# Delta rule's first step in early places and banks, key products shared through memory, and four couples at the feed-forward's entry

## The reference, cut to what matters

```python
kk = einsum("bnhcd,bnhsd->bnhcs", k, k)           # per chunk and head
a_mat = where(strict, beta[..., None] * kk * decay, 0)
t_mat = triangular_solve(eye + a_mat, eye)        # by blocks: 16, 32, 64, 128 here
qk = einsum("bnhcd,bnhsd->bnhcs", q, k) * decay
def step(state, xs):                              # one chunk after another, forward and backward
    v_new = u - w @ state
    o = q_c @ state + qk_c @ v_new
    state = state * exp(gl) + k_c.T @ v_new
h = h + concat([attn, gdn]) @ w_out
h = h + square(relu(rmsnorm(h) @ w_ffn_in)) @ w_ffn_out
```

## Time and profile before

| | |
|---|---|
| median of 3 runs | 2490.85 us |
| profiled execution | 2490.52 us |
| its span | 2488.7 us |
| TensorE busy | 2378.4 us (96%) |
| VectorE, ScalarE, GpSimd busy | 1424.9, 1031.3, 1042.4 us |
| granted clock, mean | 0.983 |

### The profile page before, as it was taken

How to read it: one execution, slowest core, us unless ns; L and a number is a source line. 1 busy time by engine, 2 the same in 40 slices (tenths; PEclk the granted TensorE clock), 3 DMA queues, 4 the chain that set the end, 5 groups by cost and what they waited for, 6 DMA issues and landing times. The chain is left out here.

```text
span 2488.7 us, 31195 instructions
## 1 busy us (share of the span) xinstructions
PE 2378.4 (96%) x11797; PEld 1902.7 (76%) x11797; DVE 1424.9 (57%) x1866; ACT 1031.3 (41%) x1748; POOL 1042.4 (42%) x647
## 2 busy tenths in 40 slices
PE   8999889998979999999999999999999999999986
PEld 6778778876857888878888777777777788877765
DVE  7754166555587555588667576666647441115854
ACT  5651144455244555544446243434333321015532
POOL 2112156453357666646767221212122342126553
PEclk9999999999998999999999999999999999999998
DMA  4113221115313444665553312111111452246462
GB/s 154 43 53 112 76 81 48 44 48 169 106 55 141 155 148 150 215 227 165 161 153 106 115 43 68 51 57 54 68 43 60 156 178 94 93 142 200 157 207 77
DMA packets 141202, 278.59 MB, mean 112 GB/s; under 512 B 26579, under 2 KB 36051, under 8 KB 141052
## 3 DMA queue, kind: packets, MB, share of 16 engines
q1 hardware_dynamic: 141052, 276.59, 33.3%
HBM read 200.18 MB, written 76.37 MB: 111 GB/s over the span
## 5 line engine op out<-in xcount | busy, mean ns | idle before, releaser
L1798 POOL TENSOR_TENSOR t<-t,t 128x512 fp32r<-128x512 f32 (+1 forms) x431 | 744.1, 1733 | 1145.7 <-ACT t L858 1127.6
L550 PE MATMUL bank<-t,t 128*128 128x512 f32 x1840 | 741.2, 403 | 18.5 <-ACT t L858 14.6
L552 PE MATMUL bank<-t,t 128*128 128x512 f32 x1840 | 722.1, 392 | 5.3 <-POOL t L1798 5.0
L554 PE MATMUL bank<-t,t 128*128 128x512 f32 x1840 | 722.0, 392 | 0.4 <-POOL t L1798 0.4
L858 ACT ACTIVATE t<-t 128x512 fp32r<-128x512 f32 (+1 forms) x581 | 398.4, 708 | 777.0 <-PE bank L554 390.4
L550 PEld LDWEIGHTS bank<-t,t 128*128 128x128 f32 x1840 | 348.3, 189 | 98.1 <-issue 29.5
L552 PEld LDWEIGHTS bank<-t,t 128*128 128x128 f32 x1840 | 348.3, 189 | 83.4 <-POOL t L1798 10.2
L554 PEld LDWEIGHTS bank<-t,t 128*128 128x128 f32 x1840 | 347.8, 189 | 75.9 <-POOL t L1798 1.2
L752 PE MATMUL bank<-t,t 128*128 128x512 f32 x896 | 351.9, 393 | 19.5 <-ACT t L858 18.7
L756 PE MATMUL bank<-t,t 128*128 128x512 f32 x896 | 351.8, 393 | 8.8 <-DVE t L1232 5.5
L754 PE MATMUL bank<-t,t 128*128 128x512 f32 x896 | 351.1, 392 | 1.6 <-POOL t L1798 1.6
(11 more groups left out here) (213 smaller groups left out, 2503.7 us busy)
## 6 DMA issues: line engine op xcount, KB each, us to landing
t<-in_w SPq DMA_DIRECT2D x87, 512.0 KB, 3.7
hid_scr<-t SPq DMA_DIRECT2D x112, 256.0 KB, 2.3
t<-hid_scr SPq DMA_DIRECT2D x112, 256.0 KB, 2.7
t<-in_wf SPq DMA_DIRECT2D x80, 256.0 KB, 3.4
g_scr<-t SPq DMA_DIRECT2D x36, 512.0 KB, 2.6
t<-g_scr SPq DMA_DIRECT2D x72, 256.0 KB, 3.4
t<-in_wf SPq DMA_DIRECT2D x35, 512.0 KB, 4.4
t<-in_wo SPq DMA_DIRECT2D x24, 512.0 KB, 3.8
```

The source lines that it names most:

```text
L550: e.matmul(ps[:, :], hi[:, w, :], XH[:, x, hs], start=k == 0, stop=False)
L552: e.matmul(ps[:, :], lo[:, w, :], XH[:, x, hs], start=False, stop=False)
L554: last = e.matmul(ps[:, :], hi[:, w, :], XL[:, x, hs], start=False, stop=k == j.nk - 1)
L1798: return e.tensor_tensor(out, x, high.bitcast(F32), ALU.subtract)
```

## The change

1. Step 0 of both directions gets buffers of its own (`unit`, `first`) at 180 and 202 to 218 KB, which P1 leaves early, and preparation moves to banks 3 to 5, the chain to 0 and 1, attention to 2, 6 and 7. Step 0's loads wait for the weight copies of tiles 21 and 22 only. The list `p1_end` falls into `p1_x` (last matmul) and `p1_banks` (with the evacuations), and the z stores stand only with those who write over z.
2. `kk` leaves TensorE: each (d, i) loads the product from `kk_scr` (`kkl`) into one buffer, kkL. `a1` multiplies beta by it, `a2` by D.
3. `qk` is made for i < 4 alone, copied out by ScalarE (`qkc`), written to a scratch (`qk_out`) and read by the other direction's steps 4 to 7 (`qk_in`).
4. `EARLY = 4`. After t = 0, 2 of four couples and t = 6 of two, couples 0 and 1 go in turns through t = 1, 3, 4, 5, then couples 2 and 3 through these and 6. The early weights lie at 180, 184, 168 and 152 KB, so `wpair` of couple 1 waits for P3's last weight copies alone, and `ws` of couples 0 and 1 has rank 0.7 (1.3 before).
5. `x2lp`, `txp` and `tlp`, 4 + 4 + 8 instructions on GpSimd, go to VectorE.

```diff
-EARLY = 3
+EARLY = 4
+PAIR_TURNS = [(i, t) for t in (0, 2) for i in range(EARLY)] + [(0, 6), (1, 6)]
+PAIR_TURNS += [(g + i, t) for g in (0, 2) for t in ((1, 3, 4, 5, 6) if g else (1, 3, 4, 5)) for i in range(2)]
...
+        self.qk_scr, self.kkL = scratch("qk_scr", [8, 128, 512]), at(220.5, [128, 4, 128])
+        first = [dict(P=180, QK=218), dict(EB=208, D=210, T=210, AT=212, TT=214, P=202, QK=216)]
+    def unit(self, d, i, name):
+        if i == 0 and name in self.first[d]:
+            return self.first[d][name]
+        return self.U[d][name][i % 2]
...
-        self.pre = [self.raw[1], self.raw[0], at(168, [128, 8, 128])]
+        self.pre = [at(o, [128, 8, 128]) for o in (180, 184, 168, 152)]
...
-            put("P3", 23 + m, 0, 8, ("Y",), 0, half, "h", (3, m), 4)
+            put("P3", 23 + m, 0, 8, ("Y",), 0, half, "h", (3, m), 4, (3, 2, 0, 1) * 4)
...
     def prep_bank(*step):
-        return banks[p.bank(*step)]
+        return banks[3 + p.bank(*step)]
     def chain_bank(*step):
-        return banks[3 + p.bank(*step)]
+        return banks[p.bank(*step)]
-    def kk(d, i):
-        heads(prep_bank("kk", d, i), lambda j: M.kF[:, j, c], lambda j: M.kF[:, j, c]).then_inc(*tick("kk", d, i))
...
+    def qkc(d, i):
+        q.wait_ge(done("qk", d, i))
+        if i:
+            q.wait_ge(*[done(*x) for x in K.p1_banks], *[done("z_out", h) for h in (2, 3)], done("lb", 0, 0, TOP))
+        out = M.oF[:, :, 128 * n:128 * n + 128] if i else M.unit(d, 0, "QK")[:, :, :]
+        copy(out, v4(K.prep_bank("qk", d, i))).then_inc(*tick("qkc", d, i))
...
     def a1(d, i):
-        q.wait_ge(done("ebx", d, i), done("bel", d, i))
-        tt(AT, AT, D, ALU.mult)
+        q.wait_ge(done("kkl", d, i), done("bel", d, i))
+        tt(AT, AT, M.kkL[:, :, :], ALU.mult)
     def a2(d, i):
-        q.wait_ge(done("kk", d, i), done("a1", d, i))
-        tt(AT, AT, v4(K.prep_bank("kk", d, i)), ALU.mult)
+        q.wait_ge(done("ebx", d, i), done("a1", d, i))
+        tt(AT, AT, D, ALU.mult)
...
     def wpair(i, r):
         elif i == 1:
-            q.wait_ge(*[done(x, K.turn[1 - r, t]) for t in (0, 2) for x in ("vh", "vl")])
+            q.wait_ge(done("whi", 30 - r), done("wlo", 30 - r))
...
     def gcl(d, i):
-        else:
-            q.wait_ge(*[done(*y) for y in K.p1_end])
+        if i in (1, 2):
+            q.wait_ge(*[done(*y) for y in K.p1_x])
+        elif i == 0:
+            q.wait_ge(done("whi", 22), done("wlo", 22))
...
+    def kkl(d, i):
+        q.wait_ge(done("kk_out", n))
+        if (d, i) != (0, 0):
+            q.wait_ge(done("a1", *((0, i) if d else (1, i - 1))))
+        start(flat(M.kkL[:, :, :]), M.kk_scr[n], "kkl", d, i)
...
+    def qk_in(d, i):
+        q.wait_ge(done("qk_out", 1 - d, 7 - i), done("co", d, i - 2))
...
-        self.p1_end = [("mm", last["P1"])] + [x for b in range(last["P1"] - 2, last["P1"] + 1) for x in B.evacuations(b)]
+        self.p1_x = [("mm", last["P1"])]
+        self.p1_banks = [("mm", last["P1"])] + [x for b in range(last["P1"] - 2, last["P1"] + 1) for x in B.evacuations(b)]
...
-            add("pe", "kk", d, i, rank=r, ring="prep", frees=[("a2", (d, i))], behind=before)
+            add("sp", "kkl", d, i, rank=r)
...
+            if i < 4:
+                add("pe", "qk", d, i, rank=r, ring="prep", frees=[("qkc", (d, i))], behind=before)
+                add("act", "qkc", d, i, rank=r)
+                add("sp", "qk_out", d, i, rank=r)
+            else:
+                add("sp", "qk_in", d, i, rank=r)
...
-            add("dve", "ws", i, c, rank=1.3)
+            add("dve", "ws", i, c, rank=0.7 if i < 2 else 1.7)
-                add("pool" if h else "dve", "x2lp" if h else "x2l", h, kt, rank=1 if h == 0 else 0.4)
-        add("pool", "txp", 3, k, rank=0.5)
+                add("dve", "x2l", h, kt, rank=1)
+            add("dve", "tx", c, k, rank=r)
+            add("dve", "tl", c, k, rank=r + 0.2 * (c == 3))
```

More of the change, by code:

```diff
@@ L642, in buf @@
     def buf(d, i, name):
-        return M.U[d][name][i % 2]
-    def kk(d, i):
-        c = chunk(d, i)
-        q.wait_ge(*[done("kn", 0, h, f) for h in range(4) for f in range(2)])
-        heads(prep_bank("kk", d, i), lambda j: M.kF[:, j, c], lambda j: M.kF[:, j, c]).then_inc(*tick("kk", d, i))
+        return M.unit(d, i, name)
     def qk(d, i):
@@ L720, in aqk @@
             lo = 64 * g
-            last = e.matmul(banks[5 + g][:, 0:128 * (s1 - s0)], M.qaB[lo:lo + 64, j, :], M.kaF[lo:lo + 64, S - 128 * s1:S - 128 * s0], start=True, stop=True)
+            last = e.matmul(banks[2 + 4 * g][:, 0:128 * (s1 - s0)], M.qaB[lo:lo + 64, j, :], M.kaF[lo:lo + 64, S - 128 * s1:S - 128 * s0], start=True, stop=True)
         last.then_inc(*tick("aqk", n, j))
@@ L1002, in ltt @@
     def ltt(d, i, l):
[L1003 removed]
+        n, TT, ps = i if d == 0 else 7 - i, M.unit(d, i, "TT"), K.prep_bank("lx", d, i, l)
         q.wait_ge(done("lx", d, i, l))
@@ L1014, in cn @@
         if i == 0:
-            q.wait_ge(*[done(*x) for x in K.p1_end])
+            q.wait_ge(*[done(*x) for x in K.p1_x])
         else:
@@ L1539, in tx, with tl @@
             h = 1 if c == 1 else 0
[L1540 removed]
+            q.wait_ge(done("tx", 2, k), done("x2h", h, k + 4), done("x2l", h, k + 4))
             tt(x(k + 4, h), x(k + 4, h), x(k, 0), ALU.subtract).then_inc(*tick("tx", c, k))
[L1543 to L1546 removed]
+    def tl(c, k):
+        m, h = {3: (k, 1), 2: (k, 0), 1: (k + 4, 1), 4: (k + 4, 0)}[c]
+        hi, lo = (M.XH[:, k, HALF[1]], M.XL[:, k, HALF[1]]) if c == 3 else (x[:, k, :] for x in M.T[c])
+        q.wait_ge(done("th", c, k), done("tx", c, k))
+        early = {(1, 2): 3, (1, 3): 3, (4, 2): 2, (4, 3): 2, (2, 0): 0, (2, 1): 0, (2, 2): 1, (2, 3): 1}.get((c, k))
+        if early is not None:
+            q.wait_ge(*[done(x, K.turn[early, t]) for t in (0, 2) for x in ("vh", "vl")])
+        low(lo, M.H[:, m, HALF[h]], hi).then_inc(*tick("tl", c, k))
     def ws(i, c):
@@ L1973, in wpre @@
     def wpre(i):
-        q.wait_ge(*([done("whi", 29 + i), done("wlo", 29 + i)] if i < 2 else [done(*x) for x in K.p2_end]))
+        if i:
+            q.wait_ge(done("vh", K.turn[i - 1, 0]))
+        q.wait_ge(*[done(*x) for x in K.p2_end], *([done(x, 0, j) for x in ("zh", "zlo") for j in (2, 3)] if i == 3 else [done("zm", h, j) for h in range(2) for j in range(4)]))
         start(M.pre[i][:, :, :], A["wf1"][i], "wpre", i)
@@ L2095, in gcl @@
             q.wait_ge(done("lb", d, i - 2, TOP), done("sc", d, i - 2))
-        else:
-            q.wait_ge(*[done(*y) for y in K.p1_end])
-        start(flat(M.U[d]["EB"][i % 2][:, :, :]), M.row_of(64 + 8 * n + 4 * d), "gcl", d, i)
+        if i in (1, 2):
+            q.wait_ge(*[done(*y) for y in K.p1_x])
+        elif i == 0:
+            q.wait_ge(done("whi", 22), done("wlo", 22))
+        start(flat(M.unit(d, i, "EB")[:, :, :]), M.row_of(64 + 8 * n + 4 * d), "gcl", d, i)
     def bel(d, i):
@@ L2140, in hx @@
     def hx(g, h):
-        q.wait_ge(*[done(x, d, 7) for x in ("qk", "sc") for d in range(2)])
+        q.wait_ge(*[done(x, d, 7) for x in ("qkm", "sc") for d in range(2)])
         start(M.H[:, 2 * g:2 * g + 2, HALF[h]], A["xT"][:, 2 * g:2 * g + 2, HALF[h]], "hx", g, h)
@@ L2358, in prep_bank, with chain_bank @@
     def prep_bank(self, *step):
+        return self.mem.banks[3 + self.plan.bank(*step)]
+    def chain_bank(self, *step):
         return self.mem.banks[self.plan.bank(*step)]
-    def chain_bank(self, *step):
-        return self.mem.banks[3 + self.plan.bank(*step)]
     def before_head(self, g, h):
```

173 lines of the change are left out of this document (95 added, 78 removed), and 2 rows, old and new, of the table SIGNALS.

## The result

The kernel after takes 2473.26 us, the median of 4 runs (2471.70 to 2476.30), against 2491.27 us for the kernel before: 0.9934 times as long, 95% interval [0.9922, 0.9946]. It is 18 us faster where 44 were forecast, and lies 1.3 us outside the range. The profiled execution took 2472.49 us, its span is 2470.7 us.

The account below looks back on a forecast made before the run. TensorE, busy 96% of the span, was taken as the bound. Terms -21.3 - 11.5 + 1 + 3 - 15 = -43.8 from 2490.5 us gave 2446.7, said as 2447 us; range 2430 to 2472 us.

Parts of the forecast that it names:

- Products off TensorE: P2: removing sixteen key products (14.2 us) and eight query products (7.1 us) from TensorE saves 21.3 us; bounds -21.3 and 0.
- Bulk interruptions: P1: TensorE now stops at some eighteen preparation steps for VectorE or ScalarE; costs 1 us, bounds 0 and +8.
- The start of P2: Behind P1: step 0 prepared inside P1 leaves 8 of 19.5 us lost; gain 11.5 us, bounds 0 and 19.5.
- rival D: Start of P2: the early step gains nothing because step 1 waits as step 0 did; 2458.5 us, chance 0.07.
- The middle of P2: P2: a1 and a2 stay on VectorE, with 22 us of 50 free, so no cost was charged there.
- The end of P2: P2's end: with 21 us less TensorE work, chain and attention come nearer to bounding; costs 3 us, bounds 0 and +10.
- Rival A: End of P2 doesn't move with TensorE's work; attention and the chain set the pace; 2465 us, chance 0.14.
- Rival B: P2: loads through the one buffer kkL serialise the preparations, some 2578 us, mild form 2492; chance 0.08.
- The entry: Feed-forward's entry: more early couples and tiles moved to VectorE regain 15 of 29.3 us lost; bounds 0 and 25.
- Rivals C: Entry stays as long because VectorE, already full, becomes the wait with 16 more instructions; 2462 us, chance 0.12.
- The signs: P1 to entry: expected trace marks, among them hole behind P1 under 7 us, P2 about 45 us shorter, P1 15 longer.
- signs of being wrong: TensorE's waits in P1 above 5 us, P2's windows below 45 of 50 busy, or entry's hole above 12 us.

Follow-up runs that it names:

- e12: Kernel after, with key and query products both made on TensorE in every step again and multiplied out of the banks; 2494.91 us, ratio 1.0018.
- e11: Kernel after, with step 0's early places, early waits and forced orders undone, products still from memory; 2478.71 us, ratio 0.9954.
- e5: Kernel before, with only the entry's two parts added (four early couples, second input's tiles all on VectorE); 2489.44 us, ratio 0.9989.
- e10: Kernel after, with the second z store placed behind the first four gT loads, ahead of the other loads; 2474.61 us, ratio 0.9938.
- e6: Kernel after, with only the key products made on TensorE in every step again, without the load and its single buffer; 2494.20 us, ratio 1.0017.
- e9: Kernel after, with low halves and one difference of the second input's tiles back on GpSimd, four early couples kept; 2468.22 us, ratio 0.9910.
- e3: Kernel after, with squares and stores of couples 0 and 1 ranked ahead of the weight sums of couples 2 and 3; 2474.81 us, ratio 0.9935.
- e8: Kernel after, with the entry's couples going one after another instead of two side by side; 2470.50 us, ratio 0.9918.
- e15: Kernel after, with z store early, tiles back on GpSimd, and the first two couples' difference tiles and stores ranked ahead; 2468.25 us, ratio 0.9906.
- e1: Kernel after, with only attention's bias loads moved behind z's last store and the first query load; 2483.56 us, ratio 0.9973.

## Why the prediction was wrong, step by step

**Products off TensorE, -21.3: right in size** (21.6, e12). In e12's account the work behind P1 rises by 16.7 us (18.4 without the overlap) and P1 by 2.1; that the total agrees to 0.3 us is closer than its interval allows one to say. There is a condition that the prediction didn't see: with step 0 late they bring 10.7 (e11 against e5), where waits rose by 7.4 us and the clock took 3.6 more.

**Bulk interruptions, +1: right.** P1 is 15.5 us longer, of which 15.1 were expected as work, and TensorE stands no longer in it (9.2 us before, 9.5 after, nearly all in its first 50 us).

**The start of P2, -11.5: this step failed.** It said that step 1's "loads no longer stand behind the z store, 17.6 - 4.7 = 12.9 us to its first `la`". The loads don't wait for the store, but the store now waits behind the loads, and the early step had put two more users of z's place ahead of step 1. The first `lp` of the step that P2 begins with, in the kernels before (step 0) and after (step 1):
```profile
322.39 0.42 DVE L1346 TENSOR_TENSOR t<-bank,t 128x256 f32<-128x256 f32 x1
```
```profile
344.48 0.41 DVE L1370 TENSOR_TENSOR t<-bank,t 128x256 f32<-128x256 f32 x1
```
That is 25.2 us behind P1's end (297.2) before and 31.7 behind it (312.8) after. The preparation's latency behind P1 was moved to step 1 and grew, as rival D had it; idle time in the first 45 us went from 15.4 to 16.1 us, where 8 were forecast. The store explains the growth and no more: with it early (e10) 23.7 us and 11.0 us of idle time stay. The rest is step 1's own preparation. VectorE waits for its first load until 316.71 us, 3.9 us behind P1's end, and GpSimd, which the prediction named as next without a price, makes four sets of `sc` before it spreads step 1's inverse:
```profile
312.87 1.04 POOL L1883 TENSOR_TENSOR t<-t,t 128x512 f32<-128x512 f32 x1 [29.53 <-PE bank L565]
...
328.45 1.27 POOL L1861 TENSOR_TENSOR t<-t,t 128x512 f32<-128x512 f32 x1
```
No run moves these, so how the rest divides stays open. The prediction even had the move as its lower bound, 0, and took 11.5 without following step 1's chain or the order in which SyncE would issue.

**The middle of P2, 0: a term was missing.** `a1` and `a2` were said to "stay two instructions on VectorE, which has 22 us of 50 free". Spare time in the mean did not hide them: idle time there rose by 7 us (from 45 us behind P1 to 590 us, 4.2 to 11.3). The longest wait, in the kernel after, on VectorE, GpSimd and TensorE:
```profile
403.92 1.71 DVE L1362 TENSOR_TENSOR t<-t,t 128x512 f32<-128x512 f32 x1
...
408.06 2.67 DVE L1434 TENSOR_SCALAR t<-t 128x8 f32<-128x8 f32 x1
410.65 1.08 DVE L1435 TENSOR_TENSOR t<-t,t 128x8 f32<-128x8 f32 x1
411.65 1.82 DVE L1349 TENSOR_TENSOR t<-t,t 128x512 f32<-128x512 f32 x1
413.39 0.68 DVE L1362 TENSOR_TENSOR t<-t,t 128x512 f32<-128x512 f32 x1
...
402.34 2.75 POOL L1896 TENSOR_TENSOR t<-t,t 128x1536 f32<-128x1536 f32 x1 [6.27 <-DVE t L1442]
...
407.96 2.75 POOL L1896 TENSOR_TENSOR t<-t,t 128x1536 f32<-128x1536 f32 x1
...
415.06 1.12 PE L663 MATMUL bank<-t,t 128*128 128x128 f32 x4 [3.63 <-DVE t L1379]
```
The same `qkm` takes 1.71 us beside GpSimd's instruction and 0.68 in the gap between two of them; a multiplication of 128x8, whose median over eight is 0.173 us, takes 2.67 us beside one of 2.75. The instruction that TensorE waits for comes behind these in VectorE's order. The Trainium skill, GPSIMD Engine Reference, section Specifications, says that GpSimd contends with VectorE instructions that have two inputs in SBUF; 1.357 and 1.368 against 0.685 us with a bank agree. The multiplication of 128x8 has a single tensor input and is held too. Which operand comes from a bank is thus part of the price of removing a product. The prediction had the figures in its own rows and used them for the entry alone. This wait is read through; the whole 7 us are not. With both products back in the banks (e12) TensorE's idle time from P1's end to 590 us is still 25.4 us, 2.0 less than in the kernel after and 5.7 more than before. So the operands and the new loads together explain 2.0 us with step 0 early and 7.4 with it late (e5 to e11), the rest came with the early step, and what of it are operands and what are loads stays open.

**The end of P2, +3: wrong in sign, small.** Idle time from 590 us to the entry is 6.0 us after, 8.6 before. Rival A was false: P2's end follows TensorE's work. Rival B, the single buffer, doesn't show either: without it (e6) TensorE's idle time from P1's end to 590 us is 26.1 us, 1.3 less than in the kernel after.

**The entry, -15: this step failed**; it brought 2.9 in the trace. Two sub-steps did it. The comparison of "1.7 with 1.2 us" for a pair of instructions counted both engines' time, where VectorE was the full engine: the 16 tiles cost it its own place in line, and moving them back brought 5.0 us (e9). Of the two ends weighed there, the advice against moving work between these engines was the better one, if not by its reason. VectorE at the first hole, in the kernel after:
```profile
722.55 3.42 DVE L1246 TENSOR_TENSOR t<-t,t 128x512 fp32r<-128x512 f32 x2
...
727.88 1.77 DVE L1570 TENSOR_TENSOR t<-t 128x512 f32<-128x512 f32 x1
729.56 1.27 DVE L1615 TENSOR_TENSOR t<-t,bank 128x512 f32<-128x512 f32 x2
```
The sum L1615, which frees a bank, stands behind the tiles. And the third hole wasn't in the count at all: couples 0 and 1 end together, their ten stores keep SyncE for 23.4 us, and couple 2's sums wait for them:
```profile
751.71 23.40 SPq L1970 DMA_DIRECT2D hid_scr<-t  x10
...
777.65 0.69 DVE L1611 TENSOR_TENSOR t<-t,bank 128x512 f32<-128x512 f32 x1 [6.54 <-DMA hid_scr<-t]
```
e3 and e8 both closed it. With both put right the entry is 130.1 us (e15), 10.4 shorter than before; the last 4.6 of the 15 came in no run.

**The numbers.** Rivals C and D were priced each by itself, 2462 and 2458.5. Both came: 2447 + 15 + 11.5 = 2473.5, and 2473.26 was measured. That this sum agrees to 0.3 us is luck: the 7 us of waits in the middle of P2 stood in no rival, and the end of P2, which gave 2.6 us where it was to cost 3, made up for most of them. But a range that reaches to each rival alone must still hold two of them together.

**The signs.** Those for the work came: the products left P2, step 0 runs inside P1, P1 is 15.5 us longer, TensorE doesn't wait in it, and no weight sum of the first couples stands behind P3. Those for the waits failed: the hole behind P1 is 9.46 us (under 7 forecast), with the clock at 0.50 from 325 to 330 us, and the stretch from P1 to the entry is 31.3 us shorter (45 forecast). One of the signs of being wrong came, a window of P2 below 45 of 50 busy: 44.69 at 350 to 400 us.

## What to carry to other kernels

When a step is moved ahead, follow the next step from the same release: its latency is exposed in the old one's place, and every transfer that now shares the release delays the one that frees the memory. Price an operand's place with the instruction: a product read from a bank and one read from SBUF differ by a factor of two beside GpSimd. Two edits may share a hole, and then neither has a worth of its own; measure them in a square, and beside an edit of the order alone, which shows what difference counts.

## What the runs showed of the hardware

- The granted clock is part of every re-ordering: between the kernels of the table 5.6 to 12.8 us of TensorE's busy time from P1 to the entry went to it. In e1 a wait of 1.98 us was followed by 1.2 GHz (0.50 from 474 us on), as a hole of 7.09 us was in the kernel after; waits of 1.52 and 1.15 us there, at 398 to 402 us, left the clock at 1.00.
- A store of 512 KB landed in 2.6 us alone and 10.4 us behind some 3.3 MB of loads (six of 256 KB, two of 768 KB, one of 256 KB) on the same queue; 7.2 us behind 1 MB, with the rest issued after it.
- VectorE's fp32 multiplication of 128x512 takes 0.68 us with an operand in a bank, and with both in SBUF 0.68 us in a gap of GpSimd's and 1.71 us beside one of its instructions (1.36 in the mean).
